# Attention scores of two heads in one step, from the two halves of the matmul array, into the scores' bank and a transposes' bank

## The chip, the cores and the metric

One core of one Trainium2 chip. A core has engines that each run their own list of instructions in order and wait for one another by semaphores: TensorE (PE in the profile; its weight loads are PEld), VectorE (DVE), ScalarE (ACT), GpSimd (POOL) and SyncE (SP, which issues the DMA transfers). The metric is the device time of one execution in microseconds (us); lower is better.

## The reference, cut to what matters

Four transformer layers run one after the other on 256 rows of 1024 features: two layers of `first_block`, then two of `second_block`. Each has large matmuls with the weights (read once from HBM) and some small attention parts. Three of these parts have heads of 64 features, and they are what the change touches:

```python
CA_HEADS, CA_DH = 8, 64          # chunk attention, first_block
DA_HEADS, DA_DH = 4, 64          # differential attention: 2 * 4 score heads, first_block
A_Q_HEADS, A_HEAD_DIM = 16, 64   # sliding window with sinks, second_block
...
s = jnp.einsum('bqhd,bkhd->bhqk', q_i, k_i).astype(jnp.float32) + bias[None]
p = jax.nn.softmax(s, axis=-1).astype(v.dtype)
...
s = jnp.einsum('bqgd,bkgd->bgqk', q_i, k).astype(jnp.float32)
p = p[:, :, 0] - lam * p[:, :, 1]
...
scores = jnp.einsum("bnqhgd,bnkhd->bnhgqk", qb, kw).astype(jnp.float32) * (A_HEAD_DIM ** -0.5)
mx = jnp.maximum(jnp.max(scores, axis=-1, keepdims=True), sink)
den = jnp.sum(pr, axis=-1, keepdims=True) + jnp.exp(sink - mx)
```

Per head the scores are q (256 rows of 64) times k transposed, a contraction over 64, with the keys after the query's block left out. With two layers of each block that is 2 x (8 + 8 + 16) = 64 heads of scores.

## The kernel before

**Large matmuls.** The weights come as *units* of 128 x 1024 numbers. For exact float32 products each unit is split into a high part `wh` (ACT, L1212) and a low part `wl` (DVE, L1419), and PE multiplies three times: `xh` by `wh` (L1830), `xh` by `wl` (L1831), `xl` by `wh` (L1832). These are fp32r matmuls of 512 columns, 12 to a unit; units whose output has features on the partitions use L1818 to L1820, 256 columns, 24 to a unit. ACT prepares `wh` 8 units ahead, DVE `wl` behind it.

**Attention on the side.** The attention is cut into small *steps* (scores, transposes of the probabilities, product with v, and so on), and `Plan.weave` puts them between the units. How many units go between two steps is written out by hand in two strings of digits, `UNITS_AMONG_1` for the first block and `UNITS_AMONG_2` for the second, one digit for each gap. Every engine walks the same list of steps, so this list also sets the order on DVE and ACT.

**A head's scores** (`ca_s`, `da_s`, `aa_s`) are two float32 matmuls with 64 rows of contraction: query rows 128 to 255 against all 256 keys (L1903, or L1950 in `aa_s`), query rows 0 to 127 against 128 keys (L1904, L1951). A head's q and k lie transposed in `qT`, `kT` (`aqT`, `akT`): even heads on partitions 0 to 63, odd heads on 64 to 127. The output is the bank `SB` (bank 6), of which there is one. The trace shows each float32 matmul as two records (two passes).

**What follows a head's scores.** DVE reads the two pieces from `SB`, adds bias or mask, writes `Pn` (one of four slots) and takes the row maximum (L1479 and L1481, in `aa_s` L1722 and L1724), which frees `SB` (`s_done`); it negates the maximum (L1485, L1727) and counts `maxed`. ACT takes the exponential in place (L1258, L1373) and counts `soft`. PE transposes the probabilities two heads later (`probs_T`, L1886; `LAG` is 2) into one of two banks `TB` (banks 4 and 5), which take turns by a running number t for every transposing step of the program; a transpose with number t waits until t - 2 has been read (`t_done`). ACT copies the bank to `PT` (L1263), and PE multiplies with v (`ca_pv`, `da_pv`, `aa_pv`).

**A step for comparison.** `ret_s`, the retention's scores, has the same two sizes (256 and 128 columns, float32) but heads of 128 features: it uses all 128 rows of the array (L1893, L1894).

Of the kernel before, what the change touches and what calls it, by code (L numbers as in the profile page):

```python
# [10 lines left out]
ALU = mybir.AluOpType  # L11
# [4 lines left out]
P = 128  # L16
S = 256
# [19 lines left out]
UNITS_AMONG_1 = "0012211130110200212010110100101102011111010111111111112212111010110101101011411"  # L37
UNITS_AMONG_2 = "00002101110111000110101200001010110110200001102002000020300000100100411110101000101021021011"
# [258 lines left out]
def plan_block1(p, t_x):  # L297
# [95 lines left out]
    for i in range(DH + 2):  # L393
        if i >= 2:
            tt[i - 2] = p.next_t()
            p.add("probs_T", h=i - 2, t=tt[i - 2], of="da", n=q["mix", i - 2].n, slot=(2 * (i - 2)) % 4)
        if i < DH:
            for m in range(2):
                sm[2 * i + m] = p.add("da_s", g=2 * i + m, s=p.next_s(), after_t=t_d, mx=p.count("maxed"),
                                      soft=p.count("soft"))  # L400
        if 1 <= i <= DH:
            q["mix", i - 1] = p.add("da_mix", h=i - 1, n=p.count("mixed"), soft=sm[2 * i - 1].soft)
        if i >= 2:
            p.add("da_pv", h=i - 2, o=p.next_o(), t=tt[i - 2], kept=q["dv"])
# [159 lines left out]
def plan_block2(p, t_x):  # L564
# [83 lines left out]
    for i in range(AH + LAG + 1):  # L648
        if i < AH:
            sm[i] = p.add("aa_s", h=i, s=p.next_s(), after_t=t_a, mx=p.count("maxed"), soft=p.count("soft"))  # L650
        if LAG <= i < AH + LAG:
            h = i - LAG
            tt[h] = p.next_t()
            p.add("probs_T", h=h, t=tt[h], of="aa", n=sm[h].soft, slot=h % 4)
        if i > LAG:
            h = i - LAG - 1
            if h % 4 == 0:
                q["o"] = p.next_o()
            p.add("aa_pv", h=h, o=q["o"], t=tt[h], kept=q["akv"])
            if h % 4 == 3:  # L660
                p.add("aa_out", h=h, o=q["o"], soft=sm[h].soft)
# [182 lines left out]
def build(nc, plan, a):  # L844

    with ExitStack() as ctx:
# [172 lines left out]
        es, ssq, rq2 = sc2[:, 176:184], sc2[:, 184:224], sc2[:, 224:264]  # L1019
# [10 lines left out]
        steps, U = plan.steps, len(plan.units)  # L1030

# [6 lines left out]
        with nc.Block() as block:  # L1038
# [157 lines left out]
            def _(act):  # L1196
# [8 lines left out]
                for st in steps:  # L1205
# [46 lines left out]
                    elif k in ("ca_s", "da_s"):  # L1252
                        n = st.h if k == "ca_s" else st.g
                        act.wait_ge(maxed, st.mx)
                        for r in (1, 0):
                            part = b["Pn"][:, n % 4, 0:256] if r else b["Pn"][:, n % 4, 256:384]
                            at = r * CH + n if k == "ca_s" else 2 * n + r
                            last = act.activation(part, part, ACT.Exp, bias=nmx[:, 2 * (n % 8) + r:2 * (n % 8) + r + 1],  # L1258
                                                  accum_out=sm[:, at:at + 1])
                        last.then_inc(soft, 1)  # L1260
# [107 lines left out]
                    elif k == "aa_s":  # L1368
                        act.wait_ge(maxed, st.mx)
                        for r in (1, 0):  # L1370
                            part = b["Pn"][:, st.h % 4, 0:256] if r else b["Pn"][:, st.h % 4, 256:384]
                            at = 16 * r + st.h
                            last = act.activation(part, part, ACT.Exp, bias=nmx2[:, at:at + 1],  # L1373
                                                  accum_out=sm2[:, at:at + 1])
                        if st.h % 4 == 3:
                            last = act.activation(es, es, ACT.Exp)
                        last.then_inc(soft, 1)
                    elif k == "swiglu":
                        act.wait_ge(unit_done, st.c.u + 1)
                        if st.scaled:  # L1380
                            act.wait_ge(scaled, st.scaled)
                        for r in range(R):
                            act.activation(b["ffn_s"][:, st.i % 2, r, 0:st.width], DB[2 * st.c.pair + r][:, 0:st.width],  # L1383
                                           ACT.Silu, scale=root[:, r:r + 1] if st.scaled else 1.0).then_inc(silu, 1)

            @block.vector
            def _(dve):
# [26 lines left out]
                for st in steps:  # L1414
# [56 lines left out]
                    elif k in ("ca_s", "da_s"):  # L1471
                        n = st.h if k == "ca_s" else st.g
                        dve.wait_ge(s_ready, st.s + 1)
                        if k == "ca_s":
                            dve.wait_ge(bias_up, st.l + 1)
                        elif n == 0:
                            dve.wait_ge(dmask_loaded, 16)
                        add = b["bias"][:, n, :] if k == "ca_s" else b["dmask"][:, :]
                        dve.tensor_tensor_reduce(b["Pn"][:, n % 4, 0:256], SB[:, 0:256], add, 0.125, -3e38,  # L1479
                                                 ALU.add, ALU.max, mx[:, 2 * (n % 8) + 1:2 * (n % 8) + 2])  # L1480
                        dve.tensor_tensor_reduce(b["Pn"][:, n % 4, 256:384], SB[:, 256:384], add[:, 128:256],  # L1481
                                                 0.125, -3e38, ALU.add, ALU.max, mx[:, 2 * (n % 8):2 * (n % 8) + 1])\
                           .then_inc(s_done, 1)
# [232 lines left out]
                    elif k == "aa_s":  # L1716
                        dve.wait_ge(s_ready, st.s + 1)
                        n = st.h
                        if n == 0:
                            dve.wait_ge(p_masks, 16)  # L1720
                        sink = b["vec2"][:, 128 + n:129 + n]
                        dve.tensor_tensor_reduce(b["Pn"][:, n % 4, 0:256], SB[:, 0:256], b["masks"][:, 1, :],  # L1722
                                                 ADH ** -0.5, sink, ALU.add, ALU.max, mx2[:, 16 + n:17 + n])
                        dve.tensor_tensor_reduce(b["Pn"][:, n % 4, 256:384], SB[:, 256:384], b["masks"][:, 1, 128:256],  # L1724
                                                 ADH ** -0.5, sink, ALU.add, ALU.max, mx2[:, n:n + 1]).then_inc(s_done, 1)
                        dve.wait_ge(s_done, st.s + 1)
                        ins = dve.tensor_scalar(nmx2[:, n:n + 17:16], mx2[:, n:n + 17:16], -1.0, None, ALU.mult)  # L1727
                        if n % 4 == 3:
                            link(ins)
                            g = n - 3  # L1730
                            ins = dve.tensor_tensor(es.rearrange("p (r h) -> p r h", r=R),
# [3 lines left out]
                    elif k == "aa_out":  # L1735
# [5 lines left out]
                                               es.rearrange("p (r h) -> p r h", r=R), ALU.add))  # L1741
# [41 lines left out]
            def _(pe):  # L1783
# [5 lines left out]
                for st in steps:  # L1789
# [106 lines left out]
                    elif k in ("ca_s", "da_s"):  # L1896
                        if st.s:
                            pe.wait_ge(s_done, st.s)
                        turned(st.after_t)
                        n = st.h if k == "ca_s" else st.g  # L1900
# [43 lines left out]
                    elif k == "aa_s":  # L1944
                        if st.s:
                            pe.wait_ge(s_done, st.s)
                        turned(st.after_t)
                        p0 = 64 * (st.h % 2)
                        qT, kT = b["aqT"][p0:p0 + 64, st.h // 2, :], b["akT"][p0:p0 + 64, st.h // 4, :]
                        pe.matmul(SB[:, 0:256], qT[:, P:S], kT, start=True, stop=True)  # L1950
                        pe.matmul(SB[:, 256:384], qT[:, 0:P], kT[:, 0:P], start=True, stop=True).then_inc(s_ready, 1)  # L1951
# [130 lines left out]
```

## Time and profile before

| | |
|---|---|
| median of 3 runs | 2459.38 us (2456.76 to 2459.87) |
| profiled execution, its time | 2458.5 us |
| its span (first to last instruction) | 2456.7 us |
| mean granted TensorE clock | 0.992 |
| PE busy | 98% of the span |
| DVE, ACT, POOL busy | 61%, 50%, 5% |

The page of the profile has a line for each engine's busy time and a chain of work that ended last. The timeline gives, for each instruction or merged run of instructions, start and duration in us. Matmuls overlap in the pipeline, so a duration is longer than the time by which a matmul holds up the next one: that is the distance from start to start.

### The profile page before, as it was taken

The page shows a single profiled execution, that of the slowest core. Times are in us where ns is not written, and L with a number is a line of the kernel's source. Part 1 is how long each engine was busy: PE and PEld are TensorE (multiplying, and loading weights), DVE is VectorE, ACT ScalarE, POOL GpSimd, SP SyncE. Part 2 cuts the span into 40 slices and gives each one's busy share as a digit, 9 for nine tenths or more (in the row PEclk, how much of TensorE's full clock was granted, in tenths as well). Part 3 has the DMA queues.
Part 4 walks back from the last instruction along what each step waited for, and adds up shares of the span by engine and source line. Part 5 has one row for each costly group of instructions (what it writes and reads, how often), then busy time and mean ns, then how long its engine had stood idle before and what let it go on. Part 6 is the DMA issues. An engine that isn't in the chain of part 4 may idle for free.

```text
span 2456.7 us, 30447 instructions
## 1 busy us (share of the span) xinstructions
PE 2402.1 (98%) x11608; PEld 2001.8 (81%) x11608; DVE 1499.4 (61%) x2394; ACT 1216.4 (50%) x1834; POOL 113.8 (5%) x108
## 2 busy tenths in 40 slices
PE   8999999999999999899989999999999989999999
PEld 7887878877888788778878888888888878888887
DVE  5556775564557855565467756754855576657555
ACT  5555544435555354344456554544544465545443
POOL 1330000003200000000000000000000000000000
PEclk9999999999999999999999999999999999999999
DMA  7445456544454465445543444555555533435552
GB/s 298 154 163 180 154 188 235 186 161 160 155 188 157 156 224 186 163 167 197 175 166 129 146 138 171 202 187 176 206 191 192 173 130 137 155 130 205 182 192 106
DMA packets 118079, 427.56 MB, mean 174 GB/s; under 512 B 13616, under 2 KB 14384, under 8 KB 116912
## 3 DMA queue, kind: packets, MB, share of 16 engines
q1 hardware_dynamic: 117792, 425.56, 50.0%
q8 instruction: 94, 1.54, 0.2%
q14 instruction: 49, 0.40, 0.1%
q10 hardware_dynamic: 144, 0.07, 0.0%
HBM read 424.52 MB, written 1.05 MB: 173 GB/s over the span
## 4 chain that ended last, share of the span: by engine, by line
PE 94%; DVE 4%; ACT 1%; DMA 1%; issue 0%; DVEq 0%; ACTq 0%
PE bank L1830 27%; PE bank L1832 27%; PE bank L1831 26%; PE bank L1886 4%; PE bank L1818 1%; PE bank L1819 1%; PE bank L1820 1%; DMA raw<-in_weights 1%; PE bank L1950 1%; PE bank L1903 1%; PE bank L1929 0%; ACT wh L1212 0%; DVE xl L1431 0%; DVE x L1577 0%; PE bank L1964 0%
## 5 line engine op out<-in xcount | busy, mean ns | idle before, releaser
L1212 ACT ACTIVATE wh<-raw 128x1024 fp32r<-128x1024 f32 (+1 forms) x778 | 816.5, 1053 | 945.4 <-PE bank L1832 893.4
L1419 DVE TENSOR_TENSOR wl<-raw,wh 128x1024 fp32r<-128x1024 f32 (+1 forms) x778 | 943.9, 1227 | 441.5 <-ACT wh L1212 436.8
L1830 PE MATMUL bank<-wh,xh 128*128 128x512 f32 (+1 forms) x2176 | 870.7, 400 | 19.2 <-DVE xl L1431 14.2
L1832 PE MATMUL bank<-wh,xl 128*128 128x512 f32 (+1 forms) x2176 | 850.0, 391 | 0.0
L1831 PE MATMUL bank<-wl,xh 128*128 128x512 f32 (+1 forms) x2176 | 848.1, 390 | 0.0
L1830 PEld LDWEIGHTS bank<-wh,xh 128*128 128x128 f32 x2176 | 411.5, 189 | 103.1 <-issue 21.7
L1832 PEld LDWEIGHTS bank<-wh,xl 128*128 128x128 f32 x2176 | 410.9, 189 | 86.8
L1831 PEld LDWEIGHTS bank<-wl,xh 128*128 128x128 f32 x2176 | 412.2, 189 | 78.3
L1830 PE MATMUL bank<-wh,act_h 128*128 128x512 f32 x528 | 206.9, 392 | 0.0
L1832 PE MATMUL bank<-wh,act_l 128*128 128x512 f32 x528 | 205.6, 389 | 0.0
L1831 PE MATMUL bank<-wl,act_h 128*128 128x512 f32 x528 | 205.5, 389 | 0.0
L1832 PEld LDWEIGHTS bank<-wh,act_l 128*128 128x128 f32 x528 | 99.1, 188 | 20.7
L1831 PEld LDWEIGHTS bank<-wl,act_h 128*128 128x128 f32 x528 | 99.2, 188 | 20.2
L1830 PEld LDWEIGHTS bank<-wh,act_h 128*128 128x128 f32 x528 | 99.2, 188 | 20.0
L1777 DVE SCALAR_TENSOR_TENSOR ffn_a<-bank,scr,ffn_s 128x256 f32<-128x256 f32 (+1 forms) x88 | 37.8, 468 | 69.5 <-ACT ffn_s L1383 69.5
L1818 PE MATMUL bank<-xh,wh 128*128 128x256 f32 x256 | 75.5, 295 | 0.0
L1819 PE MATMUL bank<-xl,wh 128*128 128x256 f32 x256 | 73.0, 285 | 0.0
L1820 PE MATMUL bank<-xh,wl 128*128 128x256 f32 x256 | 72.9, 285 | 0.0
L1190 POOL COPY ib<-sc 128x1024 f32<-128x1024 f32 x2 | 3.8, 1908 | 1437.1 <-DVE ha_l L1431 1437.1
L1215 ACT ACTIVATE xh<-bank 128x512 fp32r<-128x512 f32 x64 | 35.2, 590 | 66.2 <-PE bank L1886 66.0
L1636 DVE SCALAR_TENSOR_TENSOR mT<-bank,convw,mT 128x255 f32<-128x255 f32 (+2 forms) x96 | 44.8, 480 | 29.1 <-ACT mT L1301 26.8
L1285 ACT ACTIVATE wide<-x 128x512 f32<-128x512 f32 x32 | 20.1, 628 | 81.0 <-DVE x L1563 41.9
(329 smaller groups left out, 2308.6 us busy)
## 6 DMA issues: line engine op xcount, KB each, us to landing
raw<-in_weights SPq DMA_DIRECT2D x760, 512.0 KB, 3.3
raw<-in_weights SPq DMA_DIRECT2D x16, 384.0 KB, 3.1
ln<-in_ln SPq DMA_DIRECT2D x4, 1024.0 KB, 6.6
bias<-in_bias SPq DMA_DIRECT2D x2, 1024.0 KB, 10.4
b_merge<-in_b_merge SPq DMA_DIRECT2D x2, 1024.0 KB, 5.5
gain<-in_gain_ffn SPq DMA_DIRECT2D x4, 512.0 KB, 3.9
decay<-in_decay SPq DMA_DIRECT2D x2, 768.0 KB, 12.0
x<-in_x SPq DMA_DIRECT2D x2, 512.0 KB, 5.1
```

The lines of the kernel that those rows point to most:

```text
L1212: act.activation(wh[:, u % NH, 0:used(u)], raw[:, u % NR, 0:used(u)], ACT.Copy).then_inc(hi_done, 1)
L1215: act.activation(split_of[st.dst][0][:, st.kg:st.kg + 4, st.tile * P:st.tile * P + P], TB[st.t % 2][:, :].rearrange("p (k n) -> p k n", k= ...
L1419: dve.tensor_tensor(wl[:, u % NR, 0:used(u)], raw[:, u % NR, 0:used(u)], wh[:, u % NH, 0:used(u)].bitcast(F32), ALU.subtract).then_inc(lo_ ...
L1636: ins = dve.scalar_tensor_tensor(t[:, back:S], DB[bank][:, 0:S - back], w[:, 3 - back:4 - back], t[:, back:S], ALU.mult, ALU.add)
L1777: ins = dve.scalar_tensor_tensor(dst, up, root[:, r:r + 1], s_in, ALU.mult, ALU.mult)
L1818: pe.matmul(out, w_h, lh[:, kt, :], start=st.first and i == 0, stop=False)
L1819: pe.matmul(out, w_h, ll[:, kt, :], start=False, stop=False)
L1820: last = pe.matmul(out, w_l, lh[:, kt, :], start=False, stop=st.last and i == st.nk - 1)
L1830: pe.matmul(out, h, w_h, start=st.first and i == 0, stop=False)
L1831: pe.matmul(out, h, w_l, start=False, stop=False)
L1832: last = pe.matmul(out, lo, w_h, start=False, stop=st.last and i == st.nk - 1)
L1886: last = pe.transpose(bank[:, i * P:(i + 1) * P], piece, ident[:, :])
```

## The change

The scores of heads h and h + 1 (h even) are made in one step. Four matmuls stand in it: 256 columns of head h from array rows 0 to 63 into `SB`, 256 columns of head h + 1 from array rows 64 to 127 into a bank `TB`, then the 128 columns of head h and those of head h + 1. The step takes a number t like a transpose, and waits for that bank. DVE handles the two heads one after the other, with one negation over four maxima; ACT takes the exponentials of both heads, counting `soft` for each. `es`, a buffer of 8 numbers a row in the windowed attention, gets a second half, as heads h + 4 may now come earlier. The digit strings lose the digits of the steps that are gone; their units stand in neighbouring gaps.

```diff
-UNITS_AMONG_1 = "0012211130110200212010110100101102011111010111111111112212111010110101101011411"
-UNITS_AMONG_2 = "00002101110111000110101200001010110110200001102002000020300000100100411110101000101021021011"
+UNITS_AMONG_1 = "10122203110202120111010010110201111101011111111111223210111011101011421"
+UNITS_AMONG_2 = "000021011101200110112000011011110200011020200002300000100100411110101000101021021011"
...
+    def scores(kind, h, t):
+        st = p.add(kind, h=h, s=p.next_s(), t=p.next_t(), after_t=t, mx=p.count("maxed"))
+        return p.count("soft"), p.count("soft")
     for i in range(CH + LAG + 1):
-        if i < CH:
-            sm[i] = p.add("ca_s", h=i, s=p.next_s(), after_t=t_c, mx=p.count("maxed"), soft=p.count("soft"))
+        if i < CH and i % 2 == 0:
+            sm[i], sm[i + 1] = scores("ca_s", i, t_c)
         if LAG <= i < CH + LAG:
             h = i - LAG
             tt[h] = p.next_t()
-            p.add("probs_T", h=h, t=tt[h], of="ca", n=sm[h].soft, slot=h % 4)
+            p.add("probs_T", h=h, t=tt[h], of="ca", n=sm[h], slot=h % 4)
...
                         act.wait_ge(maxed, st.mx)
-                        for r in (1, 0):
...
+                        for n in (st.h, st.h + 1):
+                            for r in (1, 0):
+                                part = b["Pn"][:, n % 4, 0:256] if r else b["Pn"][:, n % 4, 256:384]
...
+                            last.then_inc(soft, 1)
...
+                        for n, bank in ((st.h, SB), (st.h + 1, TB[st.t % 2])):
+                            if bank is SB:
+                                dve.wait_ge(s_ready, st.s + 1)
+                            else:
+                                dve.wait_ge(t_ready[st.t % 2], st.t // 2 + 1)
...
+                               .then_inc(s_done if bank is SB else t_done[st.t % 2], 1)
                         dve.wait_ge(s_done, st.s + 1)
-                        dve.tensor_scalar(nmx[:, 2 * (n % 8):2 * (n % 8) + 2], mx[:, 2 * (n % 8):2 * (n % 8) + 2],
-                                          -1.0, None, ALU.mult).then_inc(maxed, 1)
+                        dve.wait_ge(t_done[st.t % 2], st.t // 2 + 1)
+                        dve.tensor_scalar(nmx[:, at:at + 4], mx[:, at:at + 4], -1.0, None, ALU.mult).then_inc(maxed, 1)
...
                     elif k in ("ca_s", "da_s"):
                         if st.s:
                             pe.wait_ge(s_done, st.s)
+                        pe.wait_ge(t_done[st.t % 2], st.t // 2)
                         turned(st.after_t)
-                        n = st.h if k == "ca_s" else st.g
-                        p0 = 64 * (n % 2)
-                        qT, kT = b["qT"][p0:p0 + 64, n // 2, :], b["kT"][p0:p0 + 64, n // 2, :]
-                        pe.matmul(SB[:, 0:256], qT[:, P:S], kT, start=True, stop=True)
-                        pe.matmul(SB[:, 256:384], qT[:, 0:P], kT[:, 0:P], start=True, stop=True)\
-                          .then_inc(s_ready, 1)
+                        sides = ((0, SB, s_ready), (64, TB[st.t % 2], t_ready[st.t % 2]))
+                        for p0, bank, ready in sides:
+                            qT, kT = b["qT"][p0:p0 + 64, st.h // 2, :], b["kT"][p0:p0 + 64, st.h // 2, :]
+                            pe.matmul(bank[:, 0:256], qT[:, P:S], kT, start=True, stop=True)
+                        for p0, bank, ready in sides:
+                            qT, kT = b["qT"][p0:p0 + 64, st.h // 2, :], b["kT"][p0:p0 + 64, st.h // 2, :]
+                            pe.matmul(bank[:, 256:384], qT[:, 0:P], kT[:, 0:P], start=True, stop=True).then_inc(ready, 1)
```

`da_s` goes the same way, and `aa_s` with its own names (`aqT`, `akT`).

**PE, the first head of `ca_s` in the first layer, before.** Names are output bank, then the two operands; a head's step stands between two units.

```order
L1832 MATMUL bank1<-wh_51,xl_53 128x512
L1903 MATMUL bank6<-kT_102,qT_101 128x256 [waits t_done0,t_done1]
L1904 MATMUL bank6<-kT_102,qT_101 128x128
L1830 MATMUL bank0<-wh_51,xh_52 128x512 [waits lo_done]
L1831 MATMUL bank0<-wl_50,xh_52 128x512
```

The same place in the changed kernel; its lines L1851 to L1853 are L1830 to L1832 of before.

```order
L1853 MATMUL bank1<-wh_51,xl_53 128x512
L1925 MATMUL bank6<-kT_102,qT_101 128x256 [waits t_done0,t_done1]
L1925 MATMUL bank4<-kT_102,qT_101 128x256
L1928 MATMUL bank6<-kT_102,qT_101 128x128
L1928 MATMUL bank4<-kT_102,qT_101 128x128
L1851 MATMUL bank0<-wh_51,xh_52 128x512 [waits lo_done]
```

Where a head's two matmuls stood alone between units, four stand together, in turn between the two banks.

**PE, the third and fourth heads of `aa_s` with the first two transposes behind them, before.** `Pn` are the probabilities; L1818 begins the next unit.

```order
L1950 MATMUL bank6<-akT_116,aqT_115 128x256 [waits t_done0,t_done1,s_done]
L1951 MATMUL bank6<-akT_116,aqT_115 128x128
L1886 MATMUL bank4<-ident_55,Pn_65 128x128 [waits soft,t_done0]
L1886 MATMUL bank4<-ident_55,Pn_65 128x128 x2
L1950 MATMUL bank6<-akT_116,aqT_115 128x256 [waits t_done0,t_done1,s_done]
L1951 MATMUL bank6<-akT_116,aqT_115 128x128
L1886 MATMUL bank5<-ident_55,Pn_65 128x128 [waits soft,t_done1]
L1886 MATMUL bank5<-ident_55,Pn_65 128x128 x2
L1818 MATMUL bank0<-xh_52,wh_51 128x256 [waits lo_done]
```

And in the changed kernel (L1907 is L1886 of before):

```order
L1975 MATMUL bank6<-akT_116,aqT_115 128x256 [waits t_done1,t_done0,s_done]
L1975 MATMUL bank5<-akT_116,aqT_115 128x256
L1978 MATMUL bank6<-akT_116,aqT_115 128x128
L1978 MATMUL bank5<-akT_116,aqT_115 128x128
L1907 MATMUL bank4<-ident_55,Pn_65 128x128 [waits soft,t_done0]
L1907 MATMUL bank4<-ident_55,Pn_65 128x128 x2
L1907 MATMUL bank5<-ident_55,Pn_65 128x128 [waits soft,t_done1]
L1907 MATMUL bank5<-ident_55,Pn_65 128x128 x2
```

The second transpose writes bank 5, into which the fourth head's scores have just gone, so it waits until DVE has read them.

## Rows read from the trace of the kernel before

**Rows 1.** The page, part 1: engine, busy us, share of the span, instructions
```profile
PE 2402.1 (98%) x11608; PEld 2001.8 (81%) x11608; DVE 1499.4 (61%) x2394; ACT 1216.4 (50%) x1834; POOL 113.8 (5%) x108
```

**Rows 2.** The page, part 4: the chain that ended last, share by engine
```profile
PE 94%; DVE 4%; ACT 1%; DMA 1%; issue 0%; DVEq 0%; ACTq 0%
```

**Rows 3.** Groups of PE instructions: count, then busy us and mean ns
```profile
L1903 PE MATMUL bank<-kT,qT 64*128 64x256 f32 x64 | 22.3, 428 | 0.0
L1950 PE MATMUL bank<-akT,aqT 64*128 64x256 f32 x64 | 22.3, 428 | 0.8 <-DVE sc L1724 0.8
...
L1951 PE MATMUL bank<-akT,aqT 64*128 64x128 f32 x64 | 12.2, 270 | 0.0
L1904 PE MATMUL bank<-kT,qT 64*128 64x128 f32 x64 | 12.2, 270 | 0.0
```

**Rows 4.** PE timeline, one score step (64 rows) between units
```profile
60.04 0.39 PE L1832 MATMUL bank<-wh,xl 128*128 128x512 f32 x1
60.36 0.70 PE L1903 MATMUL bank<-kT,qT 64*128 64x256 f32 x2
60.90 0.38 PE L1904 MATMUL bank<-kT,qT 64*128 64x128 f32 x2
...
61.54 0.40 PE L1831 MATMUL bank<-wl,xh 128*128 128x512 f32 x1
61.78 0.40 PE L1832 MATMUL bank<-wh,xl 128*128 128x512 f32 x1
```

**Rows 5.** PE timeline in narrower windows: the two passes apart
```profile
60.36 0.48 PE L1903 MATMUL bank<-kT,qT 64*128 64x256 f32 x1
...
60.68 0.38 PE L1903 MATMUL bank<-kT,qT 64*128 64x256 f32 x1
```

**Rows 6.** Weight loads (PEld) around the same score step
```profile
59.82 0.19 PEld L1832 LDWEIGHTS bank<-wh,xl 128*128 128x128 f32 x1
60.36 0.29 PEld L1903 LDWEIGHTS bank<-kT,qT 64*128 64x128 f32 x2 [0.35 <-issue]
60.68 0.40 PEld L1904 LDWEIGHTS bank<-kT,qT 64*128 64x128 f32 x2
61.21 0.19 PEld L1830 LDWEIGHTS bank<-wh,xh 128*128 128x128 f32 x1
```

**Rows 7.** PE timeline, one step of `ret_s` (128 rows) between units
```profile
150.31 0.39 PE L1832 MATMUL bank<-wh,xl 128*128 128x512 f32 x1
150.54 0.59 PE L1893 MATMUL bank<-qT,kT 128*128 128x256 f32 x2
150.97 0.38 PE L1894 MATMUL bank<-qT,kT 128*128 128x128 f32 x2
...
151.42 0.39 PE L1831 MATMUL bank<-wl,xh 128*128 128x512 f32 x1
```

**Rows 8.** PE timeline, `aa_s` of heads 2 and 3 with a transpose between
```profile
1309.57 0.38 PE L1951 MATMUL bank<-akT,aqT 64*128 64x128 f32 x2
1309.88 0.55 PE L1886 MATMUL bank<-ident,Pn 128*128 128x128 f32 x3
1310.81 0.70 PE L1950 MATMUL bank<-akT,aqT 64*128 64x256 f32 x2 [0.38 <-DVE sc L1724]
```

**Rows 9.** DVE timeline, one head of `aa_s`
```profile
1309.99 0.48 DVE L1722 CUSTOM_DVE_ANT_0 Pn<-bank,masks,vec 128x256 f32<-128x256 f32 x1 [1.81 <-PE bank L1951]
...
1310.40 0.35 DVE L1724 CUSTOM_DVE_ANT_0 Pn<-bank,masks,vec 128x128 f32<-128x128 f32 x1
...
1310.79 0.17 DVE L1727 TENSOR_SCALAR sc<-sc 128x2 f32<-128x2 f32 x1
```

**Rows 10.** ACT timeline, one head's exponentials and the copy of a transpose
```profile
1312.97 0.51 ACT L1373 ACTIVATE Pn<-Pn,sc 128x256 f32<-128x256 f32 x1 [0.62 <-DVE sc L1731]
...
1313.87 0.19 ACT L1376 ACTIVATE sc<-sc 128x8 f32<-128x8 f32 x1
1313.97 0.47 ACT L1263 ACTIVATE PT<-bank 128x384 f32<-128x384 f32 x1
```

More of the change, by code:

```diff
@@ L397, in plan_block1 @@
         if i < DH:
-            for m in range(2):
-                sm[2 * i + m] = p.add("da_s", g=2 * i + m, s=p.next_s(), after_t=t_d, mx=p.count("maxed"),
-                                      soft=p.count("soft"))
+            sm[2 * i], sm[2 * i + 1] = scores("da_s", 2 * i, t_d)
         if 1 <= i <= DH:
-            q["mix", i - 1] = p.add("da_mix", h=i - 1, n=p.count("mixed"), soft=sm[2 * i - 1].soft)
+            q["mix", i - 1] = p.add("da_mix", h=i - 1, n=p.count("mixed"), soft=sm[2 * i - 1])
         if i >= 2:
@@ L648, in plan_block2 @@
     for i in range(AH + LAG + 1):
-        if i < AH:
-            sm[i] = p.add("aa_s", h=i, s=p.next_s(), after_t=t_a, mx=p.count("maxed"), soft=p.count("soft"))
+        if i < AH and i % 2 == 0:
+            p.add("aa_s", h=i, s=p.next_s(), t=p.next_t(), after_t=t_a, mx=p.count("maxed"))
+            sm[i], sm[i + 1] = p.count("soft"), p.count("soft")
         if LAG <= i < AH + LAG:
@@ L653, in plan_block2 @@
             tt[h] = p.next_t()
-            p.add("probs_T", h=h, t=tt[h], of="aa", n=sm[h].soft, slot=h % 4)
+            p.add("probs_T", h=h, t=tt[h], of="aa", n=sm[h], slot=h % 4)
         if i > LAG:
@@ L660, in plan_block2 @@
             if h % 4 == 3:
-                p.add("aa_out", h=h, o=q["o"], soft=sm[h].soft)
+                p.add("aa_out", h=h, o=q["o"], soft=sm[h])
     t_a2 = split_rows("aqk", "ha", KT, after_o=q["o"] + 1)
@@ L1252, in _ @@
                     elif k in ("ca_s", "da_s"):
-                        n = st.h if k == "ca_s" else st.g
                         act.wait_ge(maxed, st.mx)
-                        for r in (1, 0):
[L1256 to L1260, printed above, removed]
+                        for n in (st.h, st.h + 1):
+                            for r in (1, 0):
+                                part = b["Pn"][:, n % 4, 0:256] if r else b["Pn"][:, n % 4, 256:384]
+                                at = r * CH + n if k == "ca_s" else 2 * n + r
+                                last = act.activation(part, part, ACT.Exp, bias=nmx[:, 2 * (n % 8) + r:2 * (n % 8) + r + 1],
+                                                      accum_out=sm[:, at:at + 1])
+                            last.then_inc(soft, 1)
                     elif k == "probs_T":
@@ L1369, in _ @@
                         act.wait_ge(maxed, st.mx)
[L1370 to L1377, printed above, removed]
+                        for n in (st.h, st.h + 1):
+                            for r in (1, 0):
+                                part = b["Pn"][:, n % 4, 0:256] if r else b["Pn"][:, n % 4, 256:384]
+                                at = 16 * r + n
+                                last = act.activation(part, part, ACT.Exp, bias=nmx2[:, at:at + 1],
+                                                      accum_out=sm2[:, at:at + 1])
+                            if n % 4 == 3:
+                                last = act.activation(of4(es, n // 4), of4(es, n // 4), ACT.Exp)
+                            last.then_inc(soft, 1)
                     elif k == "swiglu":
@@ L1724, in _ @@
[L1724 to L1728, printed above, removed]
+                        if st.h == 0:
+                            dve.wait_ge(p_masks, 16)
@@ L1946, in _ @@
                             pe.wait_ge(s_done, st.s)
+                        pe.wait_ge(t_done[st.t % 2], st.t // 2)
                         turned(st.after_t)
[L1948 to L1951, printed above, removed]
+                        sides = ((0, SB, s_ready), (64, TB[st.t % 2], t_ready[st.t % 2]))
+                        for p0, bank, ready in sides:
+                            qT, kT = b["aqT"][p0:p0 + 64, st.h // 2, :], b["akT"][p0:p0 + 64, st.h // 4, :]
+                            pe.matmul(bank[:, 0:256], qT[:, P:S], kT, start=True, stop=True)
+                        for p0, bank, ready in sides:
+                            qT, kT = b["aqT"][p0:p0 + 64, st.h // 2, :], b["akT"][p0:p0 + 64, st.h // 4, :]
+                            pe.matmul(bank[:, 256:384], qT[:, 0:P], kT[:, 0:P], start=True, stop=True).then_inc(ready, 1)
                     elif k == "aa_pv":
```

49 lines of the change are left out of this document (29 added, 20 removed).

## The prediction

> **What bounds the kernel now.** I read the page's busy times first: PE works 98% of the span, DVE 61%, ACT 50% [rows 1]. Then the chain that ended last: 94% of it is PE [rows 2]. So whatever PE no longer does is gained nearly whole, and work on DVE or ACT counts only where PE comes to wait for it. Then the groups of PE: the score matmuls with 64 rows are four groups of 64 records, 22.3 + 22.3 + 12.2 + 12.2 = 69 us busy [rows 3]. A float32 matmul leaves two records (two passes), so 64 records are 32 heads, and L1903 and L1950 together are the 64 heads of the reference. A duration says little on a pipelined engine, so last I took the price of a step from the timeline, from start to start.
>
> **A head's scores cost PE 1.04 us now.** The last matmul of the unit before (L1832) starts at 60.04, the second of the unit behind (L1831) at 61.54 [rows 4]: 1.50 us, in which two unit matmuls have their own 0.23 each. So 1.04 us, and 64 of them are 66.6 us.
>
> **What that consists of.** `ret_s` is the control: the same 256 and 128 float32 columns, but all 128 rows. There the same distance is 150.31 to 151.42, 1.11 us [rows 7], so it costs 0.65. That is streaming alone: the two passes of 256 columns take 0.43 (150.54 to 150.97), which leaves 0.22 for the two of 128. So a pass of 256 is 0.215 and one of 128 is 0.11; with 64 rows it is the same (60.68 to 60.90 [rows 4, 5]). The other 0.39 us are paid by a 64-row visit only. The weight loads show where: normally the next load starts together with the running matmul (59.82 is before 60.04), but the first 64-row load starts only at 60.36, with 0.35 us of idle before it, and after the visit the unit's load waits until 61.21 [rows 6]. The array runs empty on the way into 64 rows and on the way back, and the first load on each side lies open.
>
> **The change, part by part.**
>
> *1. Half of the visits go.* 64 steps become 32, each still with one way in and one way out. All 64 are visits of their own now, since units, transposes or products with v stand between any two. 32 x 0.39 = 12.5 us are gained. This rests on rows directly; I would be wrong only if a change from one half to the other cost something too (rival 2).
>
> The Trainium skill says so for both: "TensorEngine Tiling (Array Packing)", section "Key Properties", has the change of the tiling mode drain the engine, and not the change of the tile within a mode. By the first half the trace agrees (0.39 us); of the second no row here shows anything.
>
> *2. The two heads may stream at the same time.* No row of before has two halves at work at once, so I bound it. One bound: nothing overlaps, four passes of 0.215 and four of 0.11, 1.30 us. The other: each pass of one half lies under one of the other, 0.65 us. Between them I take what the written order allows. It is A256, B256, A128, B128, each in two passes, and I assume that matmuls start in order and that a half takes one pass at a time. Then A's first pass runs alone (0.215), A's second and B's first together (0.215), B's second together with A's two of 128 (0.215), and B's two of 128 alone (0.22): 0.865 us, 0.43 less than in turn. The weight loads would stop it at about the same point: two loads of L1903 span 0.29 us of 0.18 each [rows 6], so they follow at 0.11, and eight of them are 0.88. Over 32 steps: 13.9 us gained in the likeliest case, 0 at one end, 20.8 at the other.
>
> I take the overlap as likelier than its absence since the halves share neither rows, nor weights, nor output bank.
>
> The Trainium skill speaks for it: "TensorE: Matmul & The Clock Gate", section "Part 3: Packing small matmuls — row/col tiling", has matmuls in different row groups run concurrently, starting about 4 ns apart, four row tiles at 3.07 times the speed, and always in order of start and end. Its model, one matmul's time plus 4 ns for each further tile, would price the pair at 0.65 us, the far end, and the time at 2427; it is rival 4. Its in-order rule is the one that my 0.865 assumes.
>
> *3. DVE and ACT.* Their work stays: the same reductions and exponentials, and 32 negations of 0.17 us fewer on DVE [rows 9], which nobody waits for. No DMA is moved past another; PE takes the weights 1% sooner; the chain has 1% of DMA in it [rows 2], so I count nothing for that. With the cover at 61% and 50% [rows 1] both keep hiding behind PE; where they don't is item 4.
>
> *4. The new waits.* Three things are later than before: a pair's maximum comes after both heads, its exponentials are four in a row ahead of the next transpose's copy on ACT, and bank `TB` is held until DVE has read head h + 1. In most places one to three units (some 2.75 us each) stand between. The tight place is the one shown for `aa_s`, heads 2 and 3, with both transposes directly behind.
> Now: the 128-column passes of head 2 start at 1309.57, so they have streamed at 1309.79; DVE starts at 1309.99 and PE gets the bank back at 1310.81 [rows 8, 9]. Without the wait PE would have gone on some 0.45 us sooner; the view calls 0.38 of it idle.
> Then: DVE needs 0.41 (1309.99 to 1310.40) plus about 0.27 for one head and 0.82 until release, so the second head lets go 0.2 + 0.68 + 0.82 = 1.7 us after the scores have streamed. The second transpose would be ready 0.1 + 0.33 us after them (L1886 starts 0.1 after 1309.79, and three transposes take 0.33). If the halves overlap, DVE starts on A's bank some 0.2 sooner. So PE waits 1.05 to 1.25 us instead of 0.45: 0.7 more, in two layers 1.4 us. Bounds: 0.8 and, should DVE be in a weight split of 1.2 us at that moment, 3.8.
> Behind the waiting transpose stands a whole unit, and the next product with v needs the first transpose's copy. ACT can start the exponentials after 1.9 us, has two heads of 0.9 (1312.97 to 1313.87) and then the copy, 0.47 [rows 10]: done at about 4.2 us. PE comes there after 1.7 + 0.33 + a unit's 2.8 = 4.8. It fits, by 0.6 us.
>
> **The sum.** 12.5 + 13.9 - 1.4 = 25.0 us. The profiled execution took 2458.5 us (span 2456.7 and 1.8 around it), so it would take 2433.5; the median of the runs is 0.9 higher, hence **2434.4 us**, 1.0% faster. What this kernel's measurement can tell from no change is about 0.2%, 5 us.
>
> **The rivals.**
> 1. *The halves run one after the other*, for instance because a float32 matmul's two passes, or the port that writes the banks, admit one matmul at a time. For it: the trace has no overlap anywhere. Against it: nothing in the profile either. The visits are still saved: 12.5 - 1.6 = 10.9, so 2448.5 us. Chance 0.22.
> 2. *Each change of half costs like a change of mode.* A step has three (A to B, B to A, A to B). If one costs what a way in or out costs, 0.39 / 2 = 0.195, a step pays 0.585 more and saves 0.39. 32 x 0.195 + 1.4 = 7.6 us slower, 2467 us. It turns the sign from 0.12 us a change upwards. For it: both ways of the mode change cost just this, and every odd and even head now pays it. Against it: the columns, rows and their number stay the same within the step. Chance 0.06.
> 3. *The overlap is there, and more of it is lost in waits than item 4 has*: at the product with v behind the tight place, at the copies behind four exponentials, or where the first product of a group waits for the output bank, whose reader on DVE now stands behind two heads. Each would be 0.3 to 1 us, in 10 to 15 places at most: 2438 to 2445 us. Against it: today L1903 (`ca_s`, `da_s`) has no idle time ahead of it at all, and L1950 (`aa_s`) 0.8 us [rows 3]. Chance 0.08.
> 4. *Full overlap*, with B's passes let past A's second: 2427 us. Chance 0.05.
>
> **How the numbers follow.** My forecast, overlap as the order allows, has 0.59, and by its own bounds (0.8 to 3.8 us of waits, streaming within 0.05 us a step) lies between 2432 and 2438. The range must reach to rival 1 to leave out less than 2 in 10: 2430 to 2450 us; rivals 2 and 4 are left out. Faster by over 0.2% are the forecast and rivals 1, 3 and 4: 0.94, less 0.03 for smaller costs of a change of half that eat most of rival 1's gain. Slower 0.06, same 0.03.
>
> **What would show it.** The distance from the unit's last matmul before a `ca_s` step to the second of the next unit, less two unit matmuls: 0.39 + 0.865 = 1.25 us if I am right, 1.69 in rival 1, 2.27 in rival 2, 1.04 in rival 4. B's first pass must start with A's second, and the idle before the first 64-row load must appear 32 times. PE should wait about 1.1 us twice, at the transpose behind `aa_s` of heads 2 and 3, for DVE. The forecast is wrong if the second bank's matmul starts only where A's has ended, or if other waits for `t_done` or `soft` over 0.5 us stand in the waits of PE.

## The result

The changed kernel takes 2426.6 us (median of 4 runs, 2425.52 to 2426.96), beside 2458.2 us for the kernel before: 31.6 us less, a ratio of 0.987 with a 95% interval of 0.9853 to 0.9888. The direction was right and the size was wrong: the forecast was 2434.4 us, and the measured time lies below the whole range of 2430 to 2450. The time is that of the rival to which I gave 0.05 (full overlap, 2427). The kernel before has 2458.2 here and 2459.4 in the table above because one more run of it is in the median.

The profile after, parts 1 and 4 of its page, answers to [rows 1, 2]: PE is busy 34 us less and still sets the end.

```profile
span 2425.2 us, 30438 instructions
...
PE 2368.5 (98%) x11608; PEld 1980.5 (82%) x11608; DVE 1491.0 (61%) x2362; ACT 1211.9 (50%) x1834; POOL 116.1 (5%) x108
...
PE 93%; DVE 5%; ACT 1%; DMA 1%; issue 1%; DVEq 0%; ACTq 0%
```

```profile
L1975 PE MATMUL bank<-akT,aqT 64*128 64x256 f32 x64 | 11.2, 428 | 0.0
L1925 PE MATMUL bank<-kT,qT 64*128 64x256 f32 x64 | 11.2, 428 | 0.0
L1978 PE MATMUL bank<-akT,aqT 64*128 64x128 f32 x64 | 6.2, 270 | 0.0
L1928 PE MATMUL bank<-kT,qT 64*128 64x128 f32 x64 | 6.2, 270 | 0.0
```

One step of the changed kernel in the timeline of PE, to lay beside [rows 4]: start, duration, count.

```profile
63.97 0.39 PE L1853 MATMUL bank<-wh,xl 128*128 128x512 f32 x1
64.29 0.70 PE L1925 MATMUL bank<-kT,qT 64*128 64x256 f32 x4
64.83 0.39 PE L1928 MATMUL bank<-kT,qT 64*128 64x128 f32 x4
65.14 0.50 PE L1851 MATMUL bank<-wh,xh 128*128 128x512 f32 x1
65.48 0.40 PE L1852 MATMUL bank<-wl,xh 128*128 128x512 f32 x1
```

From 63.97 to 65.48 are 1.51 us, less two unit matmuls of 0.23: a step of two heads costs 1.05 us, where a step of one head cost 1.04. The other steps agree with this one: PE's busy time fell by 2402.1 - 2368.5 = 33.6 us, which is 1.05 us for each of the 32 steps. Four records stand where two stood, in the same 0.70 us. In a window that ends at 64.30, two of them have already started:

```profile
64.29 0.49 PE L1925 MATMUL bank<-kT,qT 64*128 64x256 f32 x2
```

Two first passes, both 0.48 us long, together span 0.49: the second head's starts within 0.01 us of the first head's *first* pass, not with its second. In the trace this is so in all 32 steps, 0.006 or 0.007 us apart. The weight loads do the same. Against [rows 6], four of them now span 0.30 us, where two spanned 0.29:

```profile
64.29 0.30 PEld L1925 LDWEIGHTS bank<-kT,qT 64*128 64x128 f32 x4 [0.35 <-issue]
64.61 0.41 PEld L1928 LDWEIGHTS bank<-kT,qT 64*128 64x128 f32 x4
65.14 0.19 PEld L1851 LDWEIGHTS bank<-wh,xh 128*128 128x128 f32 x1
```

The way in and the way out are as they were: 0.35 us of idle ahead of the first load, and the unit's load held until the step has streamed.

The waits of PE have one new line (L1741 is DVE's second read of a bank, us in total, times, longest):

```profile
PE bank L1907 <- DVE sc L1741: 2.1, 2, 1.0
```

It stands where it was expected, at the second transpose behind `aa_s` of heads 2 and 3:

```profile
1290.23 0.39 PE L1978 MATMUL bank<-akT,aqT 64*128 64x128 f32 x4
1290.55 0.55 PE L1907 MATMUL bank<-ident,Pn 128*128 128x128 f32 x3
1292.14 0.55 PE L1907 MATMUL bank<-ident,Pn 128*128 128x128 f32 x3 [1.05 <-DVE sc L1741]
```

The sum closes. 32 x (2 x 1.04 - 1.05) = 33.0 us from the steps, less 2.1 - 0.8 = 1.3 us of waits, is 31.7; the spans differ by 2456.7 - 2425.2 = 31.5. That it closes to 0.2 us is partly luck: PE's other waits differ from one profiled execution to the next too, and a second one of the changed kernel (e10 below) had a span of 2423.2 us, 33.5 less than before.

### The profile page after: what moved, and what is told of

Its sections match the earlier page's. It is cut to its first block, busy times and chain, and to the rows that moved or that the text cites. A ratio compares the mean times of both kernels' runs of the same rounds, so it can differ in the third digit from the quotient of the medians.

```text
span 2425.2 us, 30438 instructions
## 1 busy us (share of the span) xinstructions
PE 2368.5 (98%) x11608; PEld 1980.5 (82%) x11608; DVE 1491.0 (61%) x2362; ACT 1211.9 (50%) x1834; POOL 116.1 (5%) x108
## 3 DMA queue, kind: packets, MB, share of 16 engines
HBM read 424.52 MB, written 1.05 MB: 175 GB/s over the span
## 4 chain that ended last, share of the span: by engine, by line
PE 93%; DVE 5%; ACT 1%; DMA 1%; issue 1%; DVEq 0%; ACTq 0%
PE bank L1851 27%; PE bank L1853 27%; PE bank L1852 27%; PE bank L1907 4%; PE bank L1839 1%; PE bank L1840 1%; PE bank L1841 1%; DMA raw<-in_weights 1%; DVE wl L1429 0%; PE bank L1952 0%; PE bank L1975 0%; PE bank L1925 0%; ACT wh L1221 0%; DVE xl L1441 0%; DVE x L1591 0%
## 5 line engine op out<-in xcount | busy, mean ns | idle before, releaser
L1851 PE MATMUL bank<-wh,xh 128*128 128x512 f32 (+1 forms) x2176 | 868.2, 399 | 21.1 <-DVE xl L1441 15.7
L1853 PE MATMUL bank<-wh,xl 128*128 128x512 f32 (+1 forms) x2176 | 849.6, 390 | 0.0
L1851 PEld LDWEIGHTS bank<-wh,xh 128*128 128x128 f32 x2176 | 411.0, 189 | 104.3 <-issue 23.4
L1853 PEld LDWEIGHTS bank<-wh,xl 128*128 128x128 f32 x2176 | 410.5, 189 | 86.4
L1851 PE MATMUL bank<-wh,act_h 128*128 128x512 f32 x528 | 207.0, 392 | 0.0
L1853 PE MATMUL bank<-wh,act_l 128*128 128x512 f32 x528 | 205.6, 389 | 0.0
L1853 PEld LDWEIGHTS bank<-wh,act_l 128*128 128x128 f32 x528 | 99.1, 188 | 20.7
L1851 PEld LDWEIGHTS bank<-wh,act_h 128*128 128x128 f32 x528 | 99.2, 188 | 20.0
```

The costliest lines, as they stand in the source:

```text
L1851: pe.matmul(out, h, w_h, start=st.first and i == 0, stop=False)
L1853: last = pe.matmul(out, lo, w_h, start=False, stop=st.last and i == st.nk - 1)
```

## The experiments

All are edits of the changed kernel. "A" is the head in array rows 0 to 63, "B" the one in rows 64 to 127. The price of a step is read as above, from the unit's last matmul before it to the second of the next unit, less 0.46. e1 to e4 ran beside 2459.0 us for the kernel before, e5 to e8 beside 2459.5 (one execution each), e9 to e11 beside 2457.0 (e9 one execution).

### Written head by head (e1_head_by_head)

```diff
                         for p0, bank, ready in sides:
                             qT, kT = b["qT"][p0:p0 + 64, st.h // 2, :], b["kT"][p0:p0 + 64, st.h // 2, :]
                             pe.matmul(bank[:, 0:256], qT[:, P:S], kT, start=True, stop=True)
-                        for p0, bank, ready in sides:
-                            qT, kT = b["qT"][p0:p0 + 64, st.h // 2, :], b["kT"][p0:p0 + 64, st.h // 2, :]
                             pe.matmul(bank[:, 256:384], qT[:, 0:P], kT[:, 0:P], start=True, stop=True).then_inc(ready, 1)
```

> The four matmuls of a step stand head by head: A256, A128, then B256, B128, instead of in turn. Theory 1 (each half of the array has an order of its own, and the engine looks past what waits for the other half): nothing changes, a step still costs 1.05 us between units, B's first pass starts a few ns after A's first, and the time is that of the changed kernel, 2426.6 us within 1. Theory 2 (matmuls start in the order in which they stand, and the turns of the changed kernel are what makes them overlap): B's first pass starts with A's last at the earliest, a step costs 0.39 + 1.30 - 0.11 = 1.58 us, so 32 x 0.53 = 17 us more, 2443.6 us.

Measured: 2424.9 us (2424.14 to 2425.45), 1.7 below the 2426.6 of the changed kernel where I had allowed 1; a second set of runs of the changed kernel itself (e10) gave 2425.0. Timeline of the first step:

```profile
63.19 0.39 PE L1853 MATMUL bank<-wh,xl 128*128 128x512 f32 x1
63.51 0.71 PE L1925 MATMUL bank<-kT,qT 64*128 64x256 f32 x4
64.04 0.40 PE L1926 MATMUL bank<-kT,qT 64*128 64x128 f32 x4
...
64.70 0.40 PE L1852 MATMUL bank<-wl,xh 128*128 128x512 f32 x1
```

Still 1.05 us, and all four passes of 256 columns within 0.71 us, although A's 128 columns stand ahead of B in the program. Theory 1 holds: B does not wait for what waits for A's half. It is also past the order of whole matmuls: B's first pass of L1925 starts within 0.02 us of A's first, and A's matmul of L1926, which stands ahead of it, only at 64.04. So the assumption on which my 0.865 us stood ("matmuls start in order") does not hold here.

### No overlap, the rest as it is (e2_same_half)

```diff
-                        sides = ((0, SB, s_ready), (64, TB[st.t % 2], t_ready[st.t % 2]))
+                        sides = ((0, SB, s_ready), (0, TB[st.t % 2], t_ready[st.t % 2]))
```

The second head's matmuls read the first head's q and k, so the kernel leaves out the scores of the odd heads.

> The same step, but the second head's matmuls read the first head's q and k, in the same half of the array (the odd heads' scores are those of the even ones), so nothing can overlap while the banks, the visits, the waits and DVE's and ACT's work stay. If the gain is 0.39 us a step for the visit saved and 0.65 for the overlap: a step costs 0.39 + 1.30 = 1.69 us, 32 x 0.645 = 20.6 us more than the changed kernel, 2447 us, still 11 us under the kernel before. If what made the gain was the use of a second bank or fewer waits and not the halves, it stays near 2427 us.

Measured: 2445.8 us (2444.55 to 2447.25), ratio to before 0.9948 (0.9931 to 0.9965).

```profile
62.56 0.39 PE L1853 MATMUL bank<-wh,xl 128*128 128x512 f32 x1
62.88 1.13 PE L1925 MATMUL bank<-kT,qT 64*128 64x256 f32 x4
63.85 0.60 PE L1928 MATMUL bank<-kT,qT 64*128 64x128 f32 x4
...
64.72 0.39 PE L1852 MATMUL bank<-wl,xh 128*128 128x512 f32 x1
```

1.70 us a step. This splits the gain: 2 x 1.04 - 1.70 = 0.38 us a step for the visit saved (12 us in all) and 1.70 - 1.05 = 0.65 for the overlap (21 us). The times say the same: 2459.0 - 2445.8 = 13.2 us under before, and 19 to 21 above the two medians of the changed kernel (2426.6 and, below, 2425.0). Two halves of the array are what makes the second part; two banks alone are not.

### DVE reads the transposes' bank first (e3_bank_first)

```diff
-                        for n, bank in ((st.h, SB), (st.h + 1, TB[st.t % 2])):
+                        for n, bank in ((st.h + 1, TB[st.t % 2]), (st.h, SB)):
```

> DVE reads the transposes' bank first and the scores' bank second. If the wait of PE at the second transpose behind aa_s of heads 2 and 3 (1.0 us in each of two layers) is for the bank that DVE reads second, it shrinks by one head's 0.68 us to about 0.35, 1.3 us less over two layers, 2425.3 us, which the profile shows and the times hardly. If the wait is for something else (the exponentials), it stays at 1.0 us.

Measured: 2425.3 us (2423.83 to 2427.88). The waits of PE have this line in place of 2.1, 2, 1.0:

```profile
PE bank L1907 <- DVE sc L1741: 0.8, 2, 0.4
```

0.4 us each instead of 1.05, less by the 0.65 of one head. So the wait is for the bank that DVE reads second, and DVE's time for the two heads sets its length.

### A unit between the two transposes (e4_unit_between, e11_unit_between_again)

```diff
-UNITS_AMONG_2 = "000021011101200110112000011011110200011020200002300000100100411110101000101021021011"
+UNITS_AMONG_2 = "000021011101101110112000011011110200011020200002300000100100411110101000101021021011"
```

> One digit moves in the second block: the unit that stood second between aa_s of heads 0 and 1 and aa_s of heads 2 and 3 stands between the first and the second transpose instead. The wait of 1.0 us in each of two layers goes wholly, since a unit takes 2.8 us; 2.1 us less, 2424.5 us, if the first transpose still finds its probabilities ready: its scores have ended 3.9 us before and need 1.9 + 0.9 = 2.8. If they aren't, a wait for the exponentials takes its place and nothing is gained.

Measured: 2423.4 us (2422.17 to 2424.57). The line of L1741 is gone from the waits of PE, and none for `soft`, the exponentials, has come. As 2 us is little beside the spread of single runs, it was run again beside the changed kernel itself:

> The changed kernel once more, beside the next run on the same chip: 2426.6 us within 1.5.

> The changed kernel with the one digit moved, beside the changed kernel itself: the profile of the first run showed the two waits of 1.0 us gone, so 2.1 us less than the changed kernel, 2424.5 us. A difference of over 3 us or none at all would speak against the wait as its source.

Measured: 2425.0 us (2424.46 to 2428.33) for the changed kernel (1.6 below the 2426.6 expected, where 1.5 was allowed) and 2423.4 (2422.85 to 2426.98) with the digit moved. The ranges overlap, so the times by themselves don't settle 1.6 us. That the wait of 2.1 us is gone is shown by the profile. In the profiled execution of the second run another wait, 2.5 us in e10's profile, has 6.4 us:

```profile
PE bank L1907 <- DVE x L1592: 6.4, 8, 1.1
```

It lies in the layer norm, which the digit does not touch. e4's profile, of the same kernel, has 2.5 us there, so this is a spread between executions and not an effect of the digit. It hides the gain in that one execution (2427.0 us, the slowest of the four).

### How far ahead a half is started (e5 to e7)

In the changed kernel two passes of A stand ahead of B's first, head by head four. The next three put more there.

```diff
-                            pe.matmul(bank[:, 0:256], qT[:, P:S], kT, start=True, stop=True)
+                            pe.matmul(bank[:, 0:P], qT[:, P:S], kT[:, 0:P], start=True, stop=True)
+                            pe.matmul(bank[:, P:256], qT[:, P:S], kT[:, P:S], start=True, stop=True)
```

(e5, head by head: six passes of 128 columns.)

> Head by head again, and each head's 256-column matmul is cut into two of 128, so the second head's first pass stands behind three matmuls, six passes and six weight loads of the first head. Head by head with two matmuls, it started 0.014 us after the first head's first pass; in turn, behind one matmul, 0.006. If a half takes up its own work and passing an instruction of the other half costs some 1.7 ns, B starts 0.02 us after A and the step costs 1.07 us. If looking ahead ends after the eight instructions of the run before, B starts at A's third pass or later and the step costs 1.2 us or more.

```diff
+                            for again in range(3 if p0 == 0 else 1):
+                                pe.matmul(bank[:, 0:256], qT[:, P:S], kT, start=True, stop=True)
+                                last = pe.matmul(bank[:, 256:384], qT[:, 0:P], kT[:, 0:P], start=True, stop=True)
+                            last.then_inc(ready, 1)
```

(e6, head by head: A's pair three times, 12 passes; e7: 8 in place of 3, 32 passes.)

> The first head's two matmuls are issued three times over (the same result written again), then the second head's once: 12 passes and 12 weight loads of A stand ahead of B's first. The half of A needs 3 x 0.645 = 1.94 us. If B still looks past them, it starts about 0.04 us after A and the step costs 0.39 + 1.94 = 2.33 us. If B must wait until part of A is done, it starts later, and as long as it starts within 1.29 us the step costs the same, so the start is what to read. If nothing is looked past, B starts at 1.9 us and the step costs 2.98 us.

> The same with eight times: 32 passes and 32 weight loads, 64 instructions, ahead of B's first. A's half needs 8 x 0.645 = 5.16 us. The Trainium skill, TensorE: Matmul & The Clock Gate, gives TensorE a queue of 64 instructions with a partial reorder window; if B can start only once it is within such a window, it starts late, when the first of A's have gone. Without a limit it starts 0.11 us after A. Either way the step costs 0.39 + 5.16 = 5.55 us unless B starts more than 4.5 us after A.

Measured, one execution each: 2437.1, 2470.3 and 2574.0 us; a step costs 1.38, 2.46 and 5.73 us. In e5 A's third pass (first of L1926) starts at 63.66 and B's first (L1925) at 63.67, when A's two passes of L1925 have streamed:

```profile
63.34 0.49 PE L1925 MATMUL bank<-kT,qT 64*128 64x128 f32 x2
63.66 0.27 PE L1926 MATMUL bank<-kT,qT 64*128 64x128 f32 x1
63.67 0.37 PE L1925 MATMUL bank<-kT,qT 64*128 64x128 f32 x1
```

In e6 the third repetition has four records where the first and second have two. B starts there, with the ninth of A's twelve passes:

```profile
63.64 0.70 PE L1926 MATMUL bank<-kT,qT 64*128 64x256 f32 x2
...
64.40 0.59 PE L1926 MATMUL bank<-kT,qT 64*128 64x256 f32 x2
64.83 0.38 PE L1927 MATMUL bank<-kT,qT 64*128 64x128 f32 x2
65.05 0.70 PE L1926 MATMUL bank<-kT,qT 64*128 64x256 f32 x4
65.49 0.49 PE L1927 MATMUL bank<-kT,qT 64*128 64x128 f32 x4
```

A window that ends at 65.10 shows that two of the four have started by then, where A's own two would be 0.2 us apart:

```profile
65.05 0.49 PE L1926 MATMUL bank<-kT,qT 64*128 64x256 f32 x2
```

And in e7 the eighth of eight, so with the 29th of 32:

```profile
67.22 0.59 PE L1926 MATMUL bank<-kT,qT 64*128 64x256 f32 x2
67.65 0.38 PE L1927 MATMUL bank<-kT,qT 64*128 64x128 f32 x2
67.87 0.70 PE L1926 MATMUL bank<-kT,qT 64*128 64x256 f32 x4
```

With 6, 12 and 32 passes ahead, B starts each time together with A's fourth pass from the end: four have not yet streamed. With two or four ahead it starts at once. B starts 0.33, 1.42 and 4.69 us after A, and that with the 0.39 for the visit and 0.65 for B's own streaming gives the three prices, within 0.01 us.

The number 4 fits all three. Of my expectations one did too: in e5, that looking ahead ends after eight instructions (four passes and their loads), with B at A's third pass or later and 1.2 us or more. Unlimited looking ahead, none at all and one as far as 64 instructions don't fit, and in e6 I had not expected B to start so late that the step costs more than A's 2.33 us.

It is not a number of columns: e1 and e5 both have 768 columns of A ahead, in four and in six passes, and only in e5 does B wait. Whether the hardware counts passes, passes with their loads (eight instructions), or float32 matmuls (two) these runs don't tell apart.

### Thirds in turn (e9_thirds_in_turn)

```diff
-                        for p0, bank, ready in sides:
-                            qT, kT = b["qT"][p0:p0 + 64, st.h // 2, :], b["kT"][p0:p0 + 64, st.h // 2, :]
-                            pe.matmul(bank[:, 0:256], qT[:, P:S], kT, start=True, stop=True)
+                        for c0 in (0, P):
+                            for p0, bank, ready in sides:
+                                qT, kT = b["qT"][p0:p0 + 64, st.h // 2, :], b["kT"][p0:p0 + 64, st.h // 2, :]
+                                pe.matmul(bank[:, c0:c0 + P], qT[:, P:S], kT[:, c0:c0 + P], start=True, stop=True)
```

> The same three matmuls of 128 columns a head as in the run with thirds head by head, where B's first pass started 0.33 us after A's and a step cost 1.39 us, but in turn (A, B, A, B, A, B). Theory now: a half is started ahead of the other's work only while at most four passes of the other half stand unfinished before it, and each half has its own stream and its own weight loads. In turn never more than two passes stand ahead, so B starts within 0.01 us of A and the step costs 0.39 + 6 x 0.11 = 1.05 us. If instead the 12 weight loads of a step share one path at 0.107 us each, the step costs 0.39 + 1.28 = 1.67 us.

Measured, one execution: 2426.3 us.

```profile
63.79 0.39 PE L1853 MATMUL bank<-wh,xl 128*128 128x512 f32 x1
64.11 0.71 PE L1926 MATMUL bank<-kT,qT 64*128 64x128 f32 x8
...
65.31 0.39 PE L1852 MATMUL bank<-wl,xh 128*128 128x512 f32 x1
```

1.52 - 0.46 = 1.06 us a step: the same twelve passes that took 1.38 head by head. Here the order in which they are written decides, where with two matmuls a head it did not. The loads, one for each 0.11 us pass in both halves at once, are no bound:

```profile
64.11 0.52 PEld L1926 LDWEIGHTS bank<-kT,qT 64*128 64x128 f32 x8 [0.35 <-issue]
```

Eight loads of 0.19 span 0.52 us; one behind the other at 0.11 they would need 0.96.

### A full-array instruction between the heads (e8_array_between)

This too is written head by head, as e1.

```diff
                             pe.matmul(bank[:, 256:384], qT[:, 0:P], kT[:, 0:P], start=True, stop=True).then_inc(ready, 1)
+                            if p0 == 0:
+                                pe.transpose(TB[st.t % 2][:, 384:512], ident[:, :], ident[:, :])
```

> Head by head, with one transpose that uses all 128 rows between the two heads (its output goes to columns of the bank that nobody reads), and one behind none. If a full-array instruction between them keeps the halves apart and each way in or out costs 0.195 us, the step costs what two visits cost and the transpose: 2 x 1.045 + 0.11 = 2.2 us. If B's half looks past the transpose too, it costs 1.05 + 0.11 = 1.16 us, or 1.55 us with a second way in and out.

Measured, one execution: 2460.3 us, where the kernel before had 2459.5.

```profile
63.67 0.39 PE L1853 MATMUL bank<-wh,xl 128*128 128x512 f32 x1
63.99 0.70 PE L1925 MATMUL bank<-kT,qT 64*128 64x256 f32 x2
64.53 0.38 PE L1926 MATMUL bank<-kT,qT 64*128 64x128 f32 x2
64.84 0.33 PE L1928 MATMUL bank<-ident 128*128 128x128 f32 x1
65.10 0.70 PE L1925 MATMUL bank<-kT,qT 64*128 64x256 f32 x2
...
66.28 0.39 PE L1852 MATMUL bank<-wl,xh 128*128 128x512 f32 x1
```

2.15 us a step, 2.2 expected. B's half lies idle while A's works, until the transpose has gone through: looking ahead stops at this instruction, which uses all rows. It also writes B's own bank, so this run by itself doesn't say which of the two holds B back. That full-array work and 64-row work stay apart with different banks too is seen at the way into the step shown above: the unit's last matmul writes bank 1, the step banks 6 and 4, and the first 64-row load still comes after 0.35 us of idle. One such transpose, 0.11 us of streaming, takes back the whole gain.

## Why the prediction was wrong

**What bounds the kernel** was right: PE keeps 98% of the span, and what the steps save there comes through whole.

**Item 1, the visits, was right.** 0.39 us each was predicted, and e2 measured 0.38. The 0.39 was read between 512-column unit matmuls only; the sign that I had set, 0.35 us of idle ahead of the first load 32 times, came at 14 of the 32 steps, as the other steps have 0.07 to 0.17 (behind a 256-column unit, a transpose or a product with v). The kernel before has the same values at those neighbours, and the fall of PE's busy time, 1.05 us a step on average, says that the total was right. Three changes of half within a step cost nothing: the two heads with no change of half in e2 pay the two ways and their streaming and no more, and the step with three (1.05) is as long as a single head's. Rival 2 is out. In this the trace agrees with the Trainium skill, "TensorEngine Tiling (Array Packing)", section "Key Properties", as the prediction quotes it.

**Item 2, the overlap, is where it failed**, in the sentence "I assume that matmuls start in order and that a half takes one pass at a time". The second half of it holds (a half's passes are 0.22 and 0.11 us apart as before), the first does not. B's first pass starts within 0.01 us of A's first, past A's second. The step of the reasoning that failed has two layers. I counted each pass as a matmul of that order; the changed kernel refutes that, though its whole matmuls still start in the written order (A256, B256, A128, B128). And e1 refutes the order of whole matmuls. So a step streams for 0.65 us and not 0.865, and the overlap brings 0.65 a step instead of 0.43: 32 x 0.215 = 6.9 us of the 7.8 by which the forecast missed. The rest, 0.9 us, is no more than medians of the same kernel differ by (2459.4 and 2458.2 before, 2426.6 and 2425.0 after). Of the prices set out beforehand (1.25, 1.69, 2.27, 1.04), the measured 1.05 is rival 4's. The second support was as weak: I read from [rows 6] that weight loads follow one another at 0.11 us, and took that for the whole array. It is so within a half; between halves they run side by side (e9). Both supports gave 0.87 by chance and so seemed to confirm each other. The far end, 0.65, was in the text as a bound, but I had left it out of the range with a chance of 0.05.

The rule of the Trainium skill that I weighed there, "TensorE: Matmul & The Clock Gate", section "Part 3: Packing small matmuls — row/col tiling", was right in its model of the span, one matmul's time and 4 ns (2427 us, measured 2426.6). The measured distance between the two starts is 6 or 7 ns in turn and 13 or 14 ns in e1. Its other sentence, that matmuls keep the program's order in start and end, is not what these float32 passes do, and in e1 not what the float32 matmuls do either; it was the one that I followed.

**Item 3** held: DVE and ACT have the same share, and no wait for either is new but the one of item 4.

**Item 4, the waits**, was right in place and size. I had 1.05 to 1.25 us twice, the profile has 1.05 and 2.1 in all; the net was 1.4 and is 1.3. Since both banks now become full at the same moment, nothing is saved by an early first bank. The other places that I feared (the product behind it, the copies behind four exponentials, the output bank) don't stand in the waits of PE, so rival 3 is out too. Rival 1 is what e2 was made to be, 2445.8 us against 2448.5.

## What to carry to other kernels

Matmuls with 64 rows of contraction pay for the way into the half-array mode and back, 0.39 us a visit between 512-column matmuls here, besides leaving half of the array idle. Put pairs from both halves side by side with no full-array instruction between; the second is then free here, down to the loads of its weights. The two had different output banks in every run; one bank for both was not tried. Write them in turn once a half has more than two float32 matmuls, since a half is started ahead only while few passes of the other stand before it (four at most in e1 and e5 to e7).

When two independent bounds agree on a number, look whether they rest on the same unproved assumption: here that what stands in one list runs in one order. And a bound that no row excludes belongs inside the range.

## What the runs showed of the hardware that I had not expected

- A float32 matmul of one half starts within 0.01 us of the other half's first pass, though that half's second pass stands before it in the program; in e1 all four passes of the first head stand before it, and both heads' four passes of 256 columns still span 0.71 us instead of 0.70.
- That reach ends: with 6, 12 and 32 passes ahead, the other half started together with the fourth pass from the end.
- Weight loads of the two halves run at the same time (8 in 0.52 us, each 0.19).
- A full-array instruction between the two halves' work keeps them wholly apart (2.15 us a step against 1.05). This one I had put at 2.2 us before the run, as one of two outcomes.
